# Turning the operands of the gate-up product in the middle steps of a float32 feed-forward layer

## The chip, the cores and the metric

The kernel runs on one core of one Trainium2 chip. The metric is the device time of the whole program in microseconds, the median of several runs. Only TensorE multiplies; VectorE (DVE), ScalarE (ACT) and GpSimd (POOL) do the rest; SyncE (SP) issues the weight transfers.

## The reference

Two transformer-like blocks run one after the other on 256 tokens of width 1024, all in float32. What the change touches is the feed-forward layer, which occurs four times (ffn1 and ffn2 in each of two layers):

```python
D_FF = 2816
def swiglu(x, w_in, w_out):          # x: 256 x 1024
    h = x @ w_in                     # w_in: 1024 x 5632
    gate, up = h[..., :D_FF], h[..., D_FF:]
    return (jax.nn.silu(gate) * up) @ w_out
x = layer_norm(ALPHA * x + 0.5 * swiglu(x, ffn_w_in[l], ffn_w_out[l]), g, b)
```

The rest (two kinds of attention, a state-space mixer with a pooling mixer, stick-breaking attention and two mixtures of experts) is not touched.

## The kernel before

Every float32 product of the dense layers is made of three TensorE matmuls (mm3, lines 657 to 661). Each operand is split into a high part, which ACT copies (fp32r), and a low part, which DVE gets as operand minus high part. high x high, high x low and low x high are added up in PSUM. The first operand of mm3 is the stationary one (loaded into the array by an LDWEIGHTS), the second one moves through it. The profile prints a matmul as out<-moving,stationary, so hh<-w_hi,xt_hi has the weights moving.

Weights come in units of 128 x 2048 floats (1 MB) through a ring of six buffers. SP loads them, waiting on unit_used. For each unit ACT makes w_hi (split, L1477), DVE makes w_lo (L1934), and PE uses it when lo_ready counts it.

A feed-forward layer is eleven steps over 256 columns of D_FF each. gated in the PE program runs a first step, then nine middle steps with step(j), j = 1 to 9 (three written out and three rounds of two in a loop; in the fourth layer all nine are written out, since parts of the later state-space mixer, s5_weights, run beside them), and a last step with an order of its own. A middle step of PE before the change is:

- tile(h_bank, half=first_half): two units of 4 x 128 rows of the input dimension; for both token tiles t of 128 tokens, x turned (xt) is stationary, 128 x 128, and 512 columns of weights (256 gate, 256 up) move. That is 2 units x 2 tiles x 4 row blocks x 3 = 48 matmuls of 512 columns. h_bank[t] holds tokens by features. first_half is raised when t = 0 is complete.
- down(j == 1, False): the product of step j-1 with w_out, 24 matmuls of 512 columns. It waits for ht_lo_ready.
- turn_h(): waits for h_ready and turns h(j) with four 128 x 128 transposes (L792) into turn_bank[0].

ACT does per step: split, silus (Silu of the gate half of each bank, L1495; the second waits for the end of the tile), split, high_h (waits for h_turned, copies the turned h out of PSUM as ht_hi, L1505), split. DVE does: split, product(t) twice (up times gate, L1966, raises h_ready), split, low_h (ht_lo = turned h minus ht_hi, L1953, raises ht_lo_ready), split. h is used by PE one step later, in down of the next step, so the step has a pipeline of its own.

In the fourth layer s5_weights puts four more transposes (L845) behind down and four ahead of the next tile for c = 0 to 3, i.e. around the turn_h of steps 6 to 9. ACT copies the first four out of turn_bank[1] (L1729, win_copied) before PE may issue the second four. After step 1 and step 2 of some layers ACT and DVE do side work of other layers (aside).

Of the kernel before, what the change touches and what calls it, by code (L numbers as in the profile page):

```python
# [26 lines left out]
P = 128  # L27
T = 256
# [101 lines left out]
def program(nc, a, out):  # L130
    with ExitStack() as ctx:
# [533 lines left out]
        def _(pe):  # L665
# [76 lines left out]
            def tile(banks, half=None, middle=None):  # L742

                for u in range(2):
# [6 lines left out]
                            mm.then_inc(half, 1)  # L751
                    mm.then_inc(unit_used, 1)

            def narrow_tile(banks):

                w = unit(KD)
                for t in range(TT):
                    for k in range(KD):
                        mm = mm3(pe, banks[t][:, 0:256], xt_part(k, t), (w[0][:, k], w[1][:, k]), k == 0, k == KD - 1)
                mm.then_inc(unit_used, 1)  # L760
# [88 lines left out]
            def gated(ready, beside=None):  # L849
                peeled = FF_PEELED if beside is None else FF_STEPS - 2  # L850

                def step(j):
                    if beside is not None:
                        beside(j, 0)
                    tile(h_bank, half=first_half)
                    if beside is not None:
                        beside(j, 1)
                    down(j == 1, False)
                    if beside is not None:
                        beside(j, 2)  # L860
                    turn_h()
                first_tile(h_bank, half=first_half, second=lambda: turn_x(1, ready=ready), by_halves=ready is None)
                turn_h()
                for j in range(1, peeled + 1):
                    step(j)
                if beside is None:
                    with seen.loop(FF_ROUNDS, [(lo_ready, 6), (h_ready, 2 * TT), (ht_lo_ready, 2)]):
                        step(FF_PEELED + 1)
                        step(FF_PEELED + 2)
                    n[0] += 6 * (FF_ROUNDS - 1)  # L870
                else:
                    beside(FF_STEPS - 1, 0)
                    pe.wait_ge(win_copied, 8)

                gate_up = []
                for u in range(2):
                    gate_up.append(unit(4))
                    mm = four(h_bank[0][:, :], gate_up[u], u, 0)
                mm.then_inc(first_half, 1)
                before = unit(2)  # L880
                pe.wait_ge(ht_lo_ready, seen(ht_lo_ready))
                for c in range(2):
                    half_down(before, 0, c, False, False)
                turn_half(0, turn_bank[0])
                half_down(before, 1, 0, False, False)
                final = unit(2)
                pe.wait_ge(ht_lo_ready, seen(ht_lo_ready))
                for c in range(2):
                    half_down(final, 0, c, False, True).then_inc(y_half, 1)
                for u in range(2):  # L890
                    four(h_bank[1][:, :], gate_up[u], u, 1).then_inc(unit_used, 1)
                half_down(before, 1, 1, False, False).then_inc(unit_used, 1)
                turn_half(1, h_bank[0])
                turn_x(0)
                pe.wait_ge(ht_lo_ready, seen(ht_lo_ready))
                half_down(final, 1, 0, False, True).then_inc(y_half, 1)
                half_down(final, 1, 1, False, True).then_inc(unit_used, 1)
# [565 lines left out]
        def _(act):  # L1463
# [29 lines left out]
            def gated(aside=(), beside=None):  # L1493
                def silu(t):
                    act.activation(gate_act[:, t], h_bank[t][:, 0:HALF], ACT.Silu).then_inc(gate_ready, 1)  # L1495

                def silus():
                    act.wait_ge(first_half, seen(first_half))
                    silu(0)
                    act.wait_ge(unit_used, seen.ahead(unit_used, 2))  # L1500
                    silu(1)

                def high_h():
                    act.wait_ge(h_turned, seen(h_turned))
                    act.activation(ht_hi[:, :, :].rearrange("p k t -> p (k t)"), turn_bank[0][:, :], ACT.Copy)\  # L1505
                        .then_inc(ht_hi_ready, 1)

                def high_half(t, bank_):
                    act.wait_ge(h_turned, seen(h_turned))
                    act.activation(ht_hi[:, :, t * P:(t + 1) * P], bank_[:, 0:2 * P].rearrange("p (k c) -> p k c", k=2),  # L1510
                                   ACT.Copy).then_inc(ht_hi_ready, 1)

                def step():
                    split()
                    silus()
                    split()
                    high_h()
                    split()
                    seen(unit_used, 3)

                high_xt(1)
                split_to(3)
                silus()
                split_to(4)
                high_h()
                seen(unit_used, 2)
                for j in range(1, (FF_PEELED if beside is None else FF_STEPS - 2) + 1):
                    ahead = peeled_splits(j)
                    split_to(ahead[0])
                    if beside is not None:  # L1530
                        beside(j, 0)
                    silus()
                    if beside is not None:
                        beside(j, 1)
                    split_to(ahead[1])
                    if beside is not None:
                        beside(j, 2)
                    high_h()
                    split_to(ahead[2])
                    seen(unit_used, 3)  # L1540
                    if j <= len(aside):
                        aside[j - 1]()
                if beside is None:
                    with seen.loop(FF_ROUNDS, [(s, 32) for s in unit_loaded] + [(unit_used, 6), (first_half, 2), (h_turned, 2)]):
                        step()
                        step()
                    n[0] += 6 * (FF_ROUNDS - 1)
                else:
                    beside(FF_STEPS - 1, 0)

                act.wait_ge(first_half, seen(first_half))
                silu(0)
                high_half(0, turn_bank[0])
                split_to(FF_UNITS + 2)
                wait_units(FF_UNITS - 2)
                silu(1)
                high_half(1, h_bank[0])
                high_xt(0)
                split_to(FF_UNITS + 3)
                stage_done(FF_UNITS)  # L1560

            def high_block(t, b, bank_):
                act.wait_ge(x_turned, seen(x_turned))
# [356 lines left out]
        def _(dve):  # L1920
# [30 lines left out]
            def low_h():  # L1951
                dve.wait_ge(ht_hi_ready, seen(ht_hi_ready))
                dve.tensor_tensor(ht_lo[:, :, :].rearrange("p k t -> p (k t)"), turn_bank[0][:, :],  # L1953
                                  ht_hi[:, :, :].bitcast(F32).rearrange("p k t -> p (k t)"), ALU.subtract)\
                    .then_inc(ht_lo_ready, 1)

            def low_half(t, bank_):
                dve.wait_ge(ht_hi_ready, seen(ht_hi_ready))
                at = (slice(None), slice(None), slice(t * P, (t + 1) * P))
                dve.tensor_tensor(ht_lo[at], bank_[:, 0:2 * P].rearrange("p (k c) -> p k c", k=2), ht_hi[at].bitcast(F32),  # L1960
                                  ALU.subtract).then_inc(ht_lo_ready, 1)

            def gated(k, aside=(), looped=True):
                def product(t):
                    dve.wait_ge(gate_ready, seen(gate_ready))
                    dve.tensor_tensor(h[:, t], h_bank[t][:, HALF:2 * HALF], gate_act[:, t], ALU.mult).then_inc(h_ready, 1)  # L1966

                def step():
                    split()
                    for t in range(TT):  # L1970
                        product(t)
                    split()
                    low_h()
                    split()

                low_xt(1)
                product(0)
# [4 lines left out]
                for j in range(1, (FF_PEELED if looped else FF_STEPS - 2) + 1):  # L1982
                    ahead = peeled_splits(j)
                    split_to(ahead[0])
                    for t in range(TT):
                        product(t)
                    split_to(ahead[1])
                    low_h()
                    split_to(ahead[2])
                    if j <= len(aside):  # L1990
                        aside[j - 1]()
                if looped:
                    with seen.loop(FF_ROUNDS, [(hi_ready, 6), (gate_ready, 2 * TT), (ht_hi_ready, 2)]):
                        step()
                        step()
                    n[0] += 6 * (FF_ROUNDS - 1)
# [870 lines left out]
```

## Time and profile before

| | |
|---|---|
| median of 3 runs | 1763.74 us (1763.15 to 1764.32) |
| the profiled execution | 1767.34 us |
| span from its first to its last instruction | 1765.5 us |
| mean granted TensorE clock | 0.988 of full |
| TensorE matmul busy | 1701.7 us, 96% |
| TensorE weight load busy | 1231.0 us, 70% |
| VectorE busy | 920.4 us, 52% |
| ScalarE busy | 631.0 us, 36% |

A matmul's duration in the trace (0.39 us for one of 512 columns) is longer than the distance to the next one, because they are pipelined; what a matmul costs is the distance from start to start.

### The profile page before, as it was taken

To read this page: it belongs to the slowest core of one execution; us is meant where nothing else is said; L and a number is where in the kernel's file an instruction comes from. 1 tells how busy PE (TensorE), PEld (TensorE's weight loads), DVE (VectorE), ACT (ScalarE), POOL (GpSimd) and SP (SyncE) were. 2 spreads that over 40 slices of the span, in tenths; PEclk is the share of its full clock that TensorE was granted. 3 is DMA by queue.
4 is the path that set the end of the run, shared out by engine and by line. 5 is a ranking of instruction groups with operands and counts; after the bars stand their busy time and mean duration, and the time that the engine had idled before them with its cause. 6 is when DMAs were issued, how large, how long until landed. Compare 5 with 4: busy or idle time off the path is not lost.

```text
span 1765.5 us, 21660 instructions
## 1 busy us (share of the span) xinstructions
PE 1701.7 (96%) x8720; PEld 1231.0 (70%) x8720; DVE 920.4 (52%) x1314; ACT 631.0 (36%) x825; POOL 107.8 (6%) x89
## 2 busy tenths in 40 slices
PE   7999999999999999999999998999998999999996
PEld 5888877778878888867887787744443777644442
DVE  4655656675555545776676587511113667511113
ACT  4544443354424443443454364211112344211110
POOL 1000060000000000332000000000000000000000
PEclk9999998999999999999999999999999999999999
DMA  7555550545555554514554352899999432999995
GB/s 293 177 189 189 196 181 6 197 184 190 190 183 197 187 181 170 211 63 171 191 184 172 122 211 102 347 418 420 427 428 410 173 143 108 357 418 427 428 426 241
DMA packets 47810, 419.77 MB, mean 238 GB/s; under 512 B 5392, under 2 KB 5392, under 8 KB 9456
## 3 DMA queue, kind: packets, MB, share of 16 engines
q1 hardware_dynamic: 44208, 405.82, 59.0%
q0 software_dynamic: 3520, 12.78, 2.1%
q8 instruction: 61, 1.00, 0.2%
q14 instruction: 21, 0.17, 0.0%
HBM read 417.53 MB, written 1.05 MB: 237 GB/s over the span
## 4 chain that ended last, share of the span: by engine, by line
PE 84%; DVE 7%; DMA 4%; ACT 3%; POOL 1%; issue 1%; SPq 0%; DVEq 0%; POOLq 0%; ACTq 0%
PE hh L1294 11%; PE y L659 10%; PE y L661 10%; PE y L660 10%; PE hh L659 8%; PE hh L661 8%; PE hh L660 8%; PE hh L1326 3%; PE turn L1204 3%; DMA wide<-pairs 3%; PE turn L1326 3%; DVE w_lo L1934 2%; PE y L1338 1%; ACT w_hi L1477 1%; PE turn L792 1%; PE y L954 1%
## 5 line engine op out<-in xcount | busy, mean ns | idle before, releaser
L1934 DVE TENSOR_TENSOR w_lo<-raw,w_hi 128x2048 fp32r<-128x2048 f32 x180 | 408.8, 2288 | 140.3 <-ACT w_hi L1477 139.6
L1477 ACT ACTIVATE w_hi<-raw 128x2048 fp32r<-128x2048 f32 x192 | 363.1, 1912 | 61.4 <-DMA raw<-units 61.3
L659 PE MATMUL hh<-w_hi,xt_hi 128*128 128x512 f32 x704 | 280.3, 398 | 8.6 <-DVE w_lo L2714 3.0
L661 PE MATMUL hh<-w_hi,xt_lo 128*128 128x512 f32 x704 | 275.9, 392 | 0.0
L660 PE MATMUL hh<-w_lo,xt_hi 128*128 128x512 f32 x704 | 275.6, 391 | 0.0
L1294 PE MATMUL hh<-wide,work 128*64 128x512 f32 x880 | 195.7, 594 | 3.1 <-DMA wide<-pairs 3.1
L659 PE MATMUL y<-w_hi,xt_hi 128*128 128x512 f32 (+1 forms) x464 | 184.0, 397 | 5.0 <-DVE xt_lo L2483 3.1
L660 PE MATMUL y<-w_lo,xt_hi 128*128 128x512 f32 (+1 forms) x464 | 179.8, 387 | 0.0
L661 PE MATMUL y<-w_hi,xt_lo 128*128 128x512 f32 (+1 forms) x464 | 179.6, 387 | 0.0
L659 PEld LDWEIGHTS hh<-w_hi,xt_hi 128*128 128x128 f32 x704 | 133.1, 189 | 37.5 <-issue 3.4
L661 PEld LDWEIGHTS hh<-w_hi,xt_lo 128*128 128x128 f32 x704 | 133.0, 189 | 28.6
L660 PEld LDWEIGHTS hh<-w_lo,xt_hi 128*128 128x128 f32 x704 | 133.2, 189 | 26.4
L1294 PEld LDWEIGHTS hh<-wide,work 128*64 128x64 f32 x880 | 61.5, 137 | 123.1 <-issue 116.8
L659 PE MATMUL y<-w_hi,ht_hi 128*128 128x512 f32 x368 | 145.0, 394 | 2.2 <-DVE w_lo L1934 2.0
L661 PE MATMUL y<-w_hi,ht_lo 128*128 128x512 f32 x368 | 143.4, 390 | 0.0
L660 PE MATMUL y<-w_lo,ht_hi 128*128 128x512 f32 x368 | 143.4, 390 | 0.0
L1495 ACT ACTIVATE gate_h<-hh 128x256 f32<-128x256 f32 x88 | 33.4, 383 | 213.7 <-PE hh L661 213.5
L659 PEld LDWEIGHTS y<-w_hi,xt_hi 128*128 128x128 f32 x464 | 88.7, 191 | 25.2 <-DVE xt_lo L2483 3.5
L599 POOL TENSOR_TENSOR rstd<-moments,minus_half 128x1 f32<-128x1 f32 x20 | 20.4, 1018 | 1330.5 <-DVE moments L2027 811.1
L661 PEld LDWEIGHTS y<-w_hi,xt_lo 128*128 128x128 f32 x464 | 88.6, 191 | 17.8
L660 PEld LDWEIGHTS y<-w_lo,xt_hi 128*128 128x128 f32 x464 | 88.9, 192 | 16.1
L2649 DVE TENSOR_TENSOR slot_mem<-hh,slot_mem 128x512 fp32r<-128x512 f32 x16 | 11.1, 691 | 142.2 <-ACT slot_mem L1861 142.2
(366 smaller groups left out, 1983.5 us busy)
## 6 DMA issues: line engine op xcount, KB each, us to landing
raw<-units SPq DMA_DIRECT2D x192, 1024.0 KB
wide<-pairs SPq DMA_DIRECT2D x81, 2048.0 KB
wide<-pairs SPq DMA_DIRECT2D x8, 1024.0 KB, 9.4
late<-pairs SPq DMA_DIRECT2D x7, 1024.0 KB
raw<-pairs SPq DMA_DIRECT2D x7, 1024.0 KB
spare<-pairs SPq DMA_DIRECT2D x2, 2048.0 KB
xt_wide<-pairs SPq DMA_DIRECT2D x2, 2048.0 KB
ln_gb<-ln_g POOLq DMA_DIRECT2D x6, 512.0 KB, 4.0
```

Of the source, the lines that this page charges most:

```text
L599: pool.tensor_tensor(rstd[:, t], moments[:, t, 1:2], minus_half[:, 0:1], ALU.pow).then_inc(rstd_ready, 1)
L659: pe.matmul(dst, left[0], right[0], start=start, stop=False)
L660: pe.matmul(dst, left[0], right[1], start=False, stop=False)
L661: return pe.matmul(dst, left[1], right[0], start=False, stop=stop)
L792: mm = pe.transpose(turn_bank[0][:, k * T + t * P:k * T + (t + 1) * P], h[:, t, k * P:(k + 1) * P], ident[:, :])
L954: mm = pe.matmul(dst, pt1[:, i % 2, c * T + kt_ * P:c * T + (kt_ + 1) * P], v1[:, kt_, cols], start=kt_ == 0, stop=kt_ == 1)
L1204: mm = pe.matmul(dst[:, k * P:(k + 1) * P], x[:, t, at * P:(at + 1) * P], pick[:, p, t, :], start=t == 0, stop=t == TT - 1)
L1294: mm = pe.matmul(dst[half(b), :], xe[:, p, 4 * u + k, half(b)], w[b][:, k, :], start=u == 0 and k == 0, stop=u == 1 and k == 3)
L1326: mm = pe.matmul(dst[half(b), :], turned[:, k, half(b)], w[b][:, k, :], start=k == 0, stop=k == 3)
L1477: act.activation(hi[r][:, :], raw[r][:, :], ACT.Copy).then_inc(hi_ready, 1)
L1495: act.activation(gate_act[:, t], h_bank[t][:, 0:HALF], ACT.Silu).then_inc(gate_ready, 1)
L1934: dve.tensor_tensor(lo[r][:, :], raw[r][:, :], hi[r][:, :].bitcast(F32), ALU.subtract)\
```

## The change

In step(j), tile is replaced by turned_tile, and turn_h by a wait for h_ready. In turned_tile the 128 x 128 blocks of weights are stationary and xt moves, all 256 tokens at once. The result is features by tokens, already in the layout that turn_h made: h_bank[0] holds the gate (m = 0, 1), h_bank[1] the up part (m = 2, 3). The tile is 2 units x 4 m x 4 k x 3 = 96 matmuls of 256 columns. ACT makes one Silu over 128 x 512 (silu_all) and copies ht_hi from h in SBUF (high_all), waiting for the end of down of the step before, since that reads ht_hi. DVE makes one product over 128 x 512 (product_all), which waits for the end of the tile, and ht_lo from h in SBUF (low_all). First and last steps keep their code, apart from waits in product(t). The core of the diff:

```diff
+            def turned_tile():
+                for u in range(2):
+                    w = unit(4)
+                    order = [(m, k) for k in range(4) for m in range(4)] if u == 0 else [(m, k) for m in range(4) for k in range(4)]
+                    for m, k in order:
+                        dst = h_bank[m // 2][:, (m % 2) * T:(m % 2 + 1) * T]
+                        mm = mm3(pe, dst, [v[:, k, m * P:(m + 1) * P] for v in w], (xt_hi[:, 4 * u + k, :], xt_lo[:, 4 * u + k, :]),
+                                 u == 0 and k == 0 and m % 2 == 0, u == 1 and k == 3 and m % 2 == 1)
+                        if u == 1 and m == 1 and k == 3:
+                            mm.then_inc(first_half, 1)
+                    mm.then_inc(unit_used, 1)
...
-                    tile(h_bank, half=first_half)
+                    turned_tile()
...
                     down(j == 1, False)
...
-                    turn_h()
+                    pe.wait_ge(h_ready, seen(h_ready))
...
+                def silu_all():
+                    act.wait_ge(first_half, seen(first_half))
+                    act.activation(gate_act.rearrange("p t c -> p (t c)"), h_bank[0], ACT.Silu).then_inc(gate_ready, 1)
+                def high_all():
+                    act.wait_ge(h_ready, seen(h_ready))
+                    act.wait_ge(unit_used, seen.ahead(unit_used, 3))
+                    act.activation(ht_hi[:, :, :].rearrange("p k t -> p (k t)"), h.rearrange("p t c -> p (t c)"), ACT.Copy)\
+                        .then_inc(ht_hi_ready, 1)
...
+                def product_all():
+                    dve.wait_ge(gate_ready, seen(gate_ready))
+                    dve.wait_ge(unit_used, seen.ahead(unit_used, 2))
+                    dve.wait_ge(ht_lo_ready, seen.ahead(ht_lo_ready, 0))
+                    dve.tensor_tensor(h.rearrange("p t c -> p (t c)"), h_bank[1], gate_act.rearrange("p t c -> p (t c)"),
+                                      ALU.mult).then_inc(h_ready, 1)
+                def low_all():
+                    dve.wait_ge(ht_hi_ready, seen(ht_hi_ready))
+                    dve.tensor_tensor(ht_lo[:, :, :].rearrange("p k t -> p (k t)"), h.rearrange("p t c -> p (t c)"),
+                                      ht_hi[:, :, :].bitcast(F32).rearrange("p k t -> p (k t)"), ALU.subtract)\
+                        .then_inc(ht_lo_ready, 1)
```

In the steps of ACT and DVE, silus, high_h, the two product(t) and low_h give way to these. The counts in the loops follow.

## Rows read from the trace of the kernel before

**Rows 1.** Page: busy time, share of the span, instructions of TensorE's matmuls.

```profile
PE 1701.7 (96%) x8720; PEld 1231.0 (70%) x8720; DVE 920.4 (52%) x1314; ACT 631.0 (36%) x825; POOL 107.8 (6%) x89
```

**Rows 2.** Page: the chain that ended last, by engine.

```profile
PE 84%; DVE 7%; DMA 4%; ACT 3%; POOL 1%; issue 1%; SPq 0%; DVEq 0%; POOLq 0%; ACTq 0%
```

**Rows 3.** Groups by line: the four transposes of turn_h; busy, mean ns | idle before.

```profile
L792 PE MATMUL turn<-ident_r,gate_h 128*128 128x128 f32 x168 | 25.3, 273 | 3.7 <-DVE gate_h L1966 3.7
```

**Rows 4.** Timeline of PE, first layer: start us, us, engine, line, out<-in.

```profile
99.66 0.39 PE L659 MATMUL hh<-w_hi,xt_hi 128*128 128x512 f32 x1
...
113.72 0.39 PE L661 MATMUL y<-w_hi,ht_lo 128*128 128x512 f32 x1
113.95 0.60 PE L792 MATMUL turn<-ident_r,gate_h 128*128 128x128 f32 x4
114.30 0.48 PE L659 MATMUL hh<-w_hi,xt_hi 128*128 128x512 f32 x1
...
130.75 0.60 PE L792 MATMUL turn<-ident_r,gate_h 128*128 128x128 f32 x4
```

**Rows 5.** Timeline of PE: turn_h of steps 2 and 9 of the first layer.

```profile
63.53 0.60 PE L792 MATMUL turn<-ident_r,gate_h 128*128 128x128 f32 x4
...
181.16 0.60 PE L792 MATMUL turn<-ident_r,gate_h 128*128 128x128 f32 x4
```

**Rows 6.** Timeline of PE: stationary weights, moving xt (state-space mixer), then 512 columns.

```profile
1047.25 0.28 PE L660 MATMUL y<-xt_lo,w_hi 128*128 128x256 f32 x1
...
1049.87 0.28 PE L661 MATMUL y<-xt_hi,w_lo 128*128 128x256 f32 x1
...
1076.14 0.28 PE L660 MATMUL hh<-xt_lo,w_hi 128*128 128x256 f32 x1
...
1081.64 0.28 PE L661 MATMUL hh<-xt_hi,w_lo 128*128 128x256 f32 x1
1081.77 0.40 PE L659 MATMUL y<-w_hi,xt_hi 128*128 128x512 f32 x1
...
1084.29 0.39 PE L661 MATMUL y<-w_hi,xt_lo 128*128 128x512 f32 x1
```

**Rows 7.** Timeline of PE: stationary xt, 256 columns of weights moving (narrow_tile).

```profile
241.69 0.28 PE L660 MATMUL y<-w_lo,xt_hi 128*128 128x256 f32 x1
...
246.37 0.28 PE L660 MATMUL y<-w_lo,xt_hi 128*128 128x256 f32 x1
```

**Rows 8.** Windows: us, busy of PE, PEld, DVE, ACT, POOL, clock, DMA, GB/s.

```profile
1076.14:1081.66 5.52, 5.52 (x48) 5.52 (x48) 4.40 (x7) 3.47 (x5) 0.00 (x0) 1.00 0.34 140
114.30:125.30 11.00, 11.00 (x51) 9.11 (x50) 5.61 (x4) 4.71 (x4) 0.00 (x0) 1.00 0.50 191
```

**Rows 9.** Timeline of PE, ACT, DVE: step 2 of the first and second layers.

```profile
45.74 0.60 PE L792 MATMUL turn<-ident_r,gate_h 128*128 128x128 f32 x4
46.38 0.60 ACT L1505 ACTIVATE ht_hi<-turn 128x512 fp32r<-128x512 f32 x1 [3.69 <-PE turn L792]
47.01 0.69 DVE L1953 TENSOR_TENSOR ht_lo<-turn,ht_hi 128x512 fp32r<-128x512 f32 x1 [1.99 <-ACT ht_hi L1505]
...
57.95 0.50 PE L659 MATMUL y<-w_hi,ht_hi 128*128 128x512 f32 x1 [0.71 <-DVE w_lo L1934]
...
368.71 0.50 PE L659 MATMUL y<-w_hi,ht_hi 128*128 128x512 f32 x1 [1.31 <-DVE w_lo L1934]
```

**Rows 10.** Timeline of PE and ACT, fourth layer: around the turn_h of step 6.

```profile
936.95 0.60 PE L792 MATMUL turn<-ident_r,gate_h 128*128 128x128 f32 x4
937.15 0.60 ACT L1729 ACTIVATE work<-turn 128x512 f32<-128x512 f32 x1 [3.03 <-PE turn L845]
...
937.80 0.66 PE L845 MATMUL turn<-ident_r,work 128*128 128x128 f32 x4 [0.25 <-ACT work L1729]
```

**Rows 11.** Timeline of ACT and DVE: the second Silu and product of that step.

```profile
108.71 0.38 ACT L1495 ACTIVATE gate_h<-hh 128x256 f32<-128x256 f32 x1 [2.34 <-PE hh L661]
...
109.12 0.43 DVE L1966 TENSOR_TENSOR gate_h<-hh,gate_h 128x256 f32<-128x256 f32 x1 [2.29 <-ACT gate_h L1495]
```

More of the change, by code:

```diff
@@ L866, in gated @@
                 if beside is None:
-                    with seen.loop(FF_ROUNDS, [(lo_ready, 6), (h_ready, 2 * TT), (ht_lo_ready, 2)]):
+                    with seen.loop(FF_ROUNDS, [(lo_ready, 6), (h_ready, 2), (ht_lo_ready, 2)]):
                         step(FF_PEELED + 1)
@@ L1514, in step @@
                     split()
-                    silus()
+                    silu_all()
                     split()
-                    high_h()
+                    high_all()
                     split()
@@ L1526, in gated @@
                 seen(unit_used, 2)
+                seen(h_ready, TT)
                 for j in range(1, (FF_PEELED if beside is None else FF_STEPS - 2) + 1):
@@ L1531, in gated @@
                         beside(j, 0)
-                    silus()
+                    silu_all()
                     if beside is not None:
@@ L1537, in gated @@
                         beside(j, 2)
-                    high_h()
+                    high_all()
                     split_to(ahead[2])
@@ L1543, in gated @@
                 if beside is None:
-                    with seen.loop(FF_ROUNDS, [(s, 32) for s in unit_loaded] + [(unit_used, 6), (first_half, 2), (h_turned, 2)]):
+                    with seen.loop(FF_ROUNDS, [(s, 32) for s in unit_loaded] + [(unit_used, 6), (first_half, 2), (h_ready, 2)]):
                         step()
@@ L1560, in gated @@
                 stage_done(FF_UNITS)
+                seen(h_ready, TT)
             def high_block(t, b, bank_):
@@ L1955, in low_h @@
                     .then_inc(ht_lo_ready, 1)
+                seen(ht_lo_ready)
             def low_half(t, bank_):
@@ L1961, in low_half @@
                                   ALU.subtract).then_inc(ht_lo_ready, 1)
+                seen(ht_lo_ready)
             def gated(k, aside=(), looped=True):
@@ L1965, in product @@
                     dve.wait_ge(gate_ready, seen(gate_ready))
+                    if seen.ahead(ht_lo_ready, 0):
+                        dve.wait_ge(ht_lo_ready, seen.ahead(ht_lo_ready, 0))
                     dve.tensor_tensor(h[:, t], h_bank[t][:, HALF:2 * HALF], gate_act[:, t], ALU.mult).then_inc(h_ready, 1)
+                def product_all():
+                    dve.wait_ge(gate_ready, seen(gate_ready))
+                    dve.wait_ge(unit_used, seen.ahead(unit_used, 2))
+                    dve.wait_ge(ht_lo_ready, seen.ahead(ht_lo_ready, 0))
+                    dve.tensor_tensor(h.rearrange("p t c -> p (t c)"), h_bank[1], gate_act.rearrange("p t c -> p (t c)"),
[5 more added lines that the diff above has]
+                        .then_inc(ht_lo_ready, 1)
+                    seen(ht_lo_ready)
                 def step():
                     split()
-                    for t in range(TT):
-                        product(t)
+                    product_all()
                     split()
-                    low_h()
+                    low_all()
                     split()
+                    seen(unit_used, 3)
+                seen(unit_used, base[0] + 2 - seen.n.get(id(unit_used), 0))
                 low_xt(1)
@@ L1984, in gated @@
                     split_to(ahead[0])
-                    for t in range(TT):
-                        product(t)
+                    product_all()
                     split_to(ahead[1])
-                    low_h()
+                    low_all()
                     split_to(ahead[2])
+                    seen(unit_used, 3)
                     if j <= len(aside):
@@ L1992, in gated @@
                 if looped:
-                    with seen.loop(FF_ROUNDS, [(hi_ready, 6), (gate_ready, 2 * TT), (ht_hi_ready, 2)]):
+                    with seen.loop(FF_ROUNDS, [(hi_ready, 6), (gate_ready, 2), (ht_hi_ready, 2), (ht_lo_ready, 2), (unit_used, 6)]):
                         step()
```

## The prediction

> **What bounds the kernel now.** I read the page's busy times first, then the chain that ended last, the groups by line, and PE's timeline through one middle step. TensorE is busy 96% of the span, and 84% of the chain is PE [rows 1, 2]. The busy share could still hide idle time behind modelled ends, so the timeline decides. In a middle step the 62 distances from 99.66 to 113.72 make 14.06 us, 0.2268 us a matmul of 512 columns, with no gap between tile and down [rows 4]. Seven steps take 181.16 - 63.53 = 117.63 us, 16.804 us each [rows 5]. 48 + 24 = 72 matmuls are 16.327 us of that. The other 0.477 us is the turn: 113.95 to 114.30 for the four transposes, 0.35 us, and 0.13 us in the slower first matmuls behind them. PE waited for the product only four times ahead of these transposes, 3.7 us in all, and those are the turns of the four first steps, which stay [rows 3]. So the middle steps are bound by what PE issues, and the sum is made of PE start-to-start distances.
>
> **The tile.** 36 middle steps (nine in each of four layers) trade 48 matmuls of 512 columns for 96 of 256. The columns that move are the same; the weight loads double. The trace of before has this very form, stationary weights with xt moving, in the state-space mixer: 46 distances from 1076.14 to 1081.64 make 5.50 us, 0.1196 us each, and this run alternates its destination between the halves of both hh banks, as the new first unit does [rows 6]. A shorter run, 22 distances from 1047.25 to 1049.87, gives 0.1191 [rows 6]; the other orientation at 256 columns gives 4.68/39 = 0.1200 [rows 7]. I take 0.1196, the longest run of the same form, with 0.1191 and 0.1200 as ends. A tile becomes 96 x 0.1196 = 11.48 us against 48 x 0.2268 = 10.89 us, +0.594 us (+0.55 to +0.63). Times 36: +21.4 us (+19.8 to +22.9).
>
> In the run of 256 columns the weight loads fill the window, 5.52 of 5.52 us, where in the 512-column tile they take 9.11 of 11.00 [rows 8]. So the load of the next weights has no slack left there. The cost behind it can be read: the first 512-column matmuls after that run come 1081.64 to 1084.29, 2.65 us for one distance of 0.12 and eleven of 0.2268 (2.61), so 0.04 us is lost where the lead is rebuilt [rows 6]. This happens between tile and down in 32 steps (in four of the fourth layer other transposes already stand there): +1.3 us (0 to +1.6).
>
> The Trainium skill ("TensorE: Matmul & The Clock Gate", Back-to-back issue gap) gives N/2.4 + 2.5 ns warm, 109.2 ns at 256 columns and 215.8 at 512. An estimate by that page would put the tile at only 96 x 0.1092 - 48 x 0.2158 = +0.12 us; the trace disagrees at both sizes (0.1196 and 0.2268), and the sum goes by the trace. The same page says that in a stream of pairs both the load and the matmul set the spacing, which agrees with the filled load row in [rows 8].
>
> **The turns.** Of 40 such turns in the feed-forward layers 36 go, and in 32 of them the whole 0.477 us goes from PE's path: -15.3 us. Bounds: -11.2 us if only the 0.35 us goes and slow first matmuls stay, -15.3 otherwise. I take the far end, since down follows tile without loss when nothing lies between [rows 4]. In the fourth layer the turns of steps 6 to 9 lie between two sets of s5 transposes. ACT's copy starts at 937.15 and releases PE at 937.80 whatever PE does meanwhile; PE was already idle 0.25 us there [rows 10]. Removing the turn lengthens that idle time: 0 us saved, four times.
>
> **Two stalls shorten.** In step 2 of the first and second layers PE waits for w_lo 0.71 and 1.31 us [rows 9]. That wait ends a chain: turn at 45.74, ACT's ht_hi at 46.38, DVE's ht_lo at 47.01, then splits and side work on DVE. Now ACT needs no turn. It starts when down has ended, about 0.2 us after 45.74 (the last down matmul starts 0.23 before and lasts 0.39), instead of 0.64 after it, so the chain comes about 0.45 us earlier, and that step shortens by 0.45 instead of growing by 0.12: -0.57 us twice, -1.1 us (0 to -1.6).
>
> **ACT and DVE.** Two Silus of 0.38 us become one of 512 columns, between 0.38 and 0.60 (ACT's 512-column copy [rows 9]); two products of 0.43 become one, 0.43 to 0.86, nearest the 0.69 us of DVE's other 512-column operation with PSUM [rows 9, 11]. I take 0.60 and 0.69. ht_hi and ht_lo from SBUF: 0.60 and 0.69 at most. product_all waits for the tile's end; before, the second product did the same through the second Silu, starting at 109.12 and ending at 109.55, 4.4 us ahead of the turn at 113.95 [rows 4, 11]. The new one needs no Silu behind the tile and ends at about 109.4. Behind it on DVE stands the next split, as before. high_all waits for down's end; behind it on ACT stands a split, which comes some 0.4 us earlier than now. All of this lies beside down (24 x 0.2268 = 5.44 us) and the next tile: 0 us. If that cover went, each step would pay the part of about 1.1 us that sticks out. SP's loads still follow unit_used at the half and the end of a tile.
>
> **Sum.** +21.4 +1.3 -15.3 -1.1 = +6.3 us: 1767.34 of the profiled execution becomes 1773.6. That execution is 3.6 us above the median of 1763.74, which becomes 1770.0 us, 0.36% slower. About 0.2%, 3.5 us, is what a measurement of this kernel can tell from no change.
>
> **Rivals.**
> - Two matmuls of 256 columns cost one of 512, since the array is bound by columns. Then the tile and its transition cost nothing and the turns and stalls alone count: -16.4, 1747.3 us, faster. For it: equal columns, and TensorE's clock stands at 1.00 in both windows, its 2.4 GHz level [rows 8]. Against it: three runs at 0.119 to 0.120. It decides below 0.1181 us a matmul, where 96 of them cost 48 of 512 plus the 0.45 us that turns, stalls and transitions give back per step; the lowest run seen is 0.1191. Chance 0.06. The page's gap above is a milder form: its +0.12 a tile would give 4.3 - 15.3 - 1.1 = -12.1 us, an estimate by that page, 1751.6.
> - The tile runs at 0.1191 and down loses nothing: 19.8 - 16.4 = +3.4, 1767.1 us, no difference that can be told. Chance 0.12.
> - The turn's time comes back as something else, a wait for h_ready or slow first matmuls at the same place: 0.13 to 0.48 us in 32 steps, +4 to +15 us on the forecast, 1774 to 1785. For it: a new wait stands where the turn was. Against it: 4.4 us of slack. Chance 0.06.
>
> **How the numbers follow.** The forecast has 0.76, its own range 1767.8 to 1772.5, from the ends of the pitch (-1.6, +1.5) and those of transition and stalls. For 8 in 10 the range takes in the second rival and the mild end of the third: 1766.3 to 1773.5. Slower by over 0.2%: 0.82; within: 0.12; faster: 0.06.
>
> **What would show it.** PE's timeline should have 256-column hh matmuls 0.1196 apart, down at 0.2268 with 0.04 lost at its start, no L792 transposes but in first steps, and a step of 11.48 + 5.44 + 0.04 = 16.96 us against 16.80. In the fourth layer steps 6 to 9 PE's idle time ahead of the second s5 transposes should grow from 0.25 to about 0.7 us. The waits on w_lo in step 2 should be near 0.15 and 0.75. A pitch under 0.118 or over 0.121, a wait on h_ready in steps 1 to 9, or any new w_lo wait would make the prediction wrong.

## The result and the profile after

The changed kernel takes 1771.12 us (median of 6 runs, 1769.73 to 1772.76) where the kernel before takes 1763.45 us (median of 6, 1761.02 to 1764.95): ratio 1.0037, 95% interval 1.0023 to 1.0052, so 4 to 9 us slower. The profiled execution took 1771.89 us, span 1770.2.

The page's busy line answers to [rows 1]: PE is as busy as before, in 1584 more matmuls, and the weight loads went from 1231.0 to 1303.9 us.

```profile
PE 1703.1 (96%) x10304; PEld 1303.9 (74%) x10304; DVE 917.5 (52%) x1278; ACT 628.5 (36%) x789; POOL 107.8 (6%) x89
```

PE's timeline through a middle step answers to [rows 4]: start us, us, engine, line, out<-in.

```profile
97.66 0.28 PE L659 MATMUL hh<-xt_hi,w_hi 128*128 128x256 f32 x1
97.77 0.28 PE L660 MATMUL hh<-xt_lo,w_hi 128*128 128x256 f32 x1
97.89 0.28 PE L661 MATMUL hh<-xt_hi,w_lo 128*128 128x256 f32 x1
...
109.05 0.28 PE L661 MATMUL hh<-xt_hi,w_lo 128*128 128x256 f32 x1
109.17 0.40 PE L659 MATMUL y<-w_hi,ht_hi 128*128 128x512 f32 x1
...
114.41 0.39 PE L661 MATMUL y<-w_hi,ht_lo 128*128 128x512 f32 x1
114.64 0.28 PE L659 MATMUL hh<-xt_hi,w_hi 128*128 128x256 f32 x1
...
131.62 0.28 PE L659 MATMUL hh<-xt_hi,w_hi 128*128 128x256 f32 x1
```

95 distances from 97.66 to 109.05 are 0.1199 us each, the tile is 11.51 us, down 5.47 us, and the step (114.64 to 131.62) 16.98 us against 16.804 before [rows 5]. No transposes stand between down and the next tile, and nothing waits there. In the window of one tile (columns as in [rows 8]) the weight loads are busy without a break:

```profile
114.64:126.15 11.51, 11.51 (x97) 11.51 (x96) 5.28 (x3) 5.23 (x5) 0.00 (x0) 1.00 0.52 182
```

The waits on w_lo in step 2 of the first and second layers, answering to [rows 9], and PE and ACT around the place of the turn of step 6 in the fourth layer, answering to [rows 10]:

```profile
58.13 0.50 PE L659 MATMUL y<-w_hi,ht_hi 128*128 128x512 f32 x1 [0.19 <-DVE w_lo L1960]
...
365.49 0.50 PE L659 MATMUL y<-w_hi,ht_hi 128*128 128x512 f32 x1 [0.81 <-DVE w_lo L1960]
...
936.88 0.60 PE L858 MATMUL turn<-ident_r,work 128*128 128x128 f32 x4
937.52 0.60 ACT L1755 ACTIVATE work<-turn 128x512 f32<-128x512 f32 x1 [3.02 <-PE turn L858]
938.26 0.30 PE L858 MATMUL turn<-ident_r,work 128*128 128x128 f32 x1 [0.78 <-ACT work L1755]
```

**Two executions compared.** The nine middle steps of the four layers, from the start of the first middle tile to the start of the last step's tile in each timeline:

| kernel | layer 1 | layer 2 | layer 3 | layer 4 | sum |
|---|---|---|---|---|---|
| before | 152.21 | 152.84 | 151.23 | 162.35 | 618.6 |
| changed | 153.35 | 153.98 | 152.90 | 165.60 | 625.8 |

That is +7.2 us, while the spans differ by 4.7 us only. The table leaves out one small gain: in the first three layers the last step no longer starts behind transposes, and its first tile part is 0.11 to 0.14 us shorter (5.44 us against 5.55 to 5.58), 0.4 us in all. Most of what is left of the difference lies in two stretches whose code is the same but for that. Their windows in before and then in the changed kernel say (us, PE busy, clock, DMA, GB/s):

```profile
181.50:325.57 144.07, 139.94 (x732) 0.95 0.36 129
...
997.50:1765.50 768.00, 732.50 (x4076) 0.99 0.77 316
```

```profile
182.56:322.09 139.53, 135.31 (x730) 0.99 0.38 133
...
999.75:1770.20 770.45, 733.18 (x4076) 0.98 0.77 315
```

In the profiled execution of before, TensorE's clock was granted at 0.95 over the first attention and it took 144.07 us; in that of the changed kernel at 0.99, and it took 139.53. Since the code there is the same and the clock differs, this part is not the change. In the last stretch it is the other way round, by 2.45 us, and 1.36 us of that stand in one place, the first tile part of the fourth layer's last step (24 matmuls of 512 columns; before, then changed, same columns as above):

```profile
997.50:1003.12 5.62, 5.62 (x25) 1.00 0.06 23
```

```profile
999.75:1006.73 6.98, 6.98 (x25) 0.78 0.05 19
```

In the changed kernel the clock falls to its lower level (1.2 GHz) there, and six distances in a row are 0.42 to 0.59 us instead of 0.22 to 0.35. PE was idle before it for 0.78 and 2.08 us, in the kernel before for 0.25 and 2.11 us. Whether the longer idle time of the changed kernel brings this on is not shown: e0, the same kernel again, has the fall at the same place (6.98 us at 0.78), e4 and e7 have it too, and e3, whose late steps are as before the change, has none, but e1, e2, e5 and e6 below, where the turn stands in these steps, have it as well.

Differences of this kind lie in the runs too (23 runs of the kernel before on one chip went from 1761.5 to 1771.9), so in the experiments the steps of the trace are read first and the ratio second.

### The profile page after: what moved, and what is told of

It reads as the page before. It is cut to its first block, busy times and chain, and to the rows that moved or that the text cites. A ratio compares the mean times of both kernels' runs of the same rounds, so it can differ in the third digit from the quotient of the medians.

```text
span 1770.2 us, 24842 instructions
## 1 busy us (share of the span) xinstructions
PE 1703.1 (96%) x10304; PEld 1303.9 (74%) x10304; DVE 917.5 (52%) x1278; ACT 628.5 (36%) x789; POOL 107.8 (6%) x89
## 4 chain that ended last, share of the span: by engine, by line
PE 84%; DVE 7%; DMA 4%; ACT 3%; issue 1%; POOL 1%; SPq 0%; DVEq 0%; POOLq 0%; ACTq 0%
PE hh L1307 11%; PE y L659 10%; PE y L660 10%; PE y L661 10%; PE hh L659 9%; PE hh L661 9%; PE hh L660 9%; DMA wide<-pairs 3%; PE hh L1339 3%; PE turn L1217 3%; PE turn L1339 3%; DVE w_lo L1960 2%; PE y L1351 1%; ACT w_hi L1490 1%; DMA raw<-units 1%
## 5 line engine op out<-in xcount | busy, mean ns | idle before, releaser
L659 PE MATMUL hh<-xt_hi,w_hi 128*128 128x256 f32 x1168 | 331.0, 283 | 0.0
L660 PE MATMUL hh<-xt_lo,w_hi 128*128 128x256 f32 x1168 | 330.5, 283 | 0.0
L661 PE MATMUL hh<-xt_hi,w_lo 128*128 128x256 f32 x1168 | 330.5, 283 | 0.0
L659 PEld LDWEIGHTS hh<-xt_hi,w_hi 128*128 128x128 f32 x1168 | 224.1, 192 | 1.2
L660 PEld LDWEIGHTS hh<-xt_lo,w_hi 128*128 128x128 f32 x1168 | 224.1, 192 | 1.1
L661 PEld LDWEIGHTS hh<-xt_hi,w_lo 128*128 128x128 f32 x1168 | 224.1, 192 | 0.0
L659 PEld LDWEIGHTS y<-w_hi,ht_hi 128*128 128x128 f32 x368 | 69.2, 188 | 16.7 <-DVE w_lo L1960 1.4
```

The source lines that it names most:

```text
L659: pe.matmul(dst, left[0], right[0], start=start, stop=False)
L660: pe.matmul(dst, left[0], right[1], start=False, stop=False)
L661: return pe.matmul(dst, left[1], right[0], start=False, stop=stop)
```

## The experiments

The diffs are shortened to their core, and in those of e2 and e4 to e7 words stand in for longer expressions of the code.

**e1: the turn put back.**

```diff
                     pe.wait_ge(h_ready, seen(h_ready))
+                    for k in range(2):
+                        for t in range(TT):
+                            pe.transpose(turn_bank[0][:, k * T + t * P:k * T + (t + 1) * P], h[:, t, k * P:(k + 1) * P], ident[:, :])
```

> The changed kernel, with four 128x128 transposes of h put back where turn_h stood in the nine middle steps (their result is read by nobody). Theory (the turn costs 0.48 us on PE's path: 0.35 for the transposes and 0.13 in the first matmuls behind them; in steps 6 to 9 of the fourth layer nothing): 32 x 0.48 = +15.3 us on the changed kernel's 1771.1, so 1786.4, ratio to the kernel before 1.013. Step in the trace 17.46 us instead of 16.98. Rival (256-column matmuls don't feel the transposes ahead of them): 32 x 0.35 = +11.2, 1782.3, step 17.33. Rival (the turn was hidden): 1771.

Measured: 1784.27 us, ratio 1.0108 (1.0085 to 1.0130). The timeline of PE:

```profile
98.52 0.60 PE L877 MATMUL turn<-ident_r,gate_h 128*128 128x128 f32 x4
98.87 0.36 PE L659 MATMUL hh<-xt_hi,w_hi 128*128 128x256 f32 x1
99.07 0.28 PE L660 MATMUL hh<-xt_lo,w_hi 128*128 128x256 f32 x1
...
115.93 0.38 PE L877 MATMUL turn<-ident_r,gate_h 128*128 128x128 f32 x2
```

The step is 17.41 us. The four transposes cost 0.35 us of PE's path, and the tile behind them 11.59 instead of 11.51, so 0.43 us: between the two forecasts, since a 256-column tile loses less behind transposes (0.08) than a 512-column one (0.13). The middle steps sum to 638.5 us, 12.6 more than the changed kernel. In the fourth layer two late steps stand 19.53 us apart (transposes at 950.54 and 970.07) against 19.60 without the turn: nothing is paid for it there. So the turn is hidden in these four steps, as the prediction had it. In step 2 of the first and second layers e1 pays next to nothing either (17.43 and 18.10 us against 17.43 and 18.06), since nobody waits for its transposes and they only fill time in which PE waits for w_lo. Where ACT's ht_hi waits for the turn, as in before and in e2, the same steps take 17.79 and 18.41 us (before) and 17.78 and 18.41 (e2).

**e2: the old operands, twice as many matmuls.**

```diff
-                    tile(h_bank, half=first_half)
+                    halved_tile(h_bank, half=first_half)     # per k, for c in range(2):
+    mm3(pe, banks[t][:, c*T:(c+1)*T], xt_part(4*u+k, t), [v[:, k, c*T:(c+1)*T] for v in w], ...)
```

> The kernel before, its operands as they were (xt stationary, weights moving), its turns in place, but each 512-column matmul of the middle tiles cut into two of 256 columns. Theory (what costs is twice as many matmuls with a 128-column load each, whichever operand is stationary): 96 x 0.1200 - 48 x 0.2268 = +0.63 us a tile, 36 x 0.63 + 36 x 0.04 behind the tile = +24 us, 1787.6, ratio 1.014; distance in the trace 0.1200. Rival (the cost comes from the exchange of operands itself, weights read by the load and xt by the moving side): no change, 1763.5.

Measured: 1784.20 us, ratio 1.0109 (1.0085 to 1.0133). PE's timeline and the window of one tile:

```profile
98.66 0.60 PE L806 MATMUL turn<-ident_r,gate_h 128*128 128x128 f32 x4
99.02 0.36 PE L659 MATMUL hh<-w_hi,xt_hi 128*128 128x256 f32 x1
...
116.08 0.38 PE L806 MATMUL turn<-ident_r,gate_h 128*128 128x128 f32 x2
```

```profile
99.02:110.61 11.59, 11.59 (x100) 11.59 (x99) 5.70 (x4) 4.69 (x4) 0.00 (x0) 1.00 0.53 183
```

The tile is 11.59 us and the step 17.42, the same as e1's to 0.01 us, though the operands stand the other way round. Which operand is stationary costs nothing; the count of matmuls and loads is what costs, and e2 doesn't tell these two apart. The forecast was 36 steps of 0.67, +24 us. Measured are 17.42 - 16.80 = 0.61 us a step, since the 256-column tile loses 0.08 us behind the transposes where a 512-column one loses 0.13, and 639.1 us for the middle steps, +20.5.

**e3: the fourth layer's steps 6 to 9 as before.** PE, ACT and DVE choose by step:

```diff
+                    turned = beside is None or j <= 5
-                    turned_tile()
+                    if turned: turned_tile()
+                    else: tile(h_bank, half=first_half)      # and turn_h, silus, product(t), high_h, low_h
```

> The changed kernel, but steps 6 to 9 of the fourth layer as in the kernel before (tile, turn_h, two Silus, two products). Theory (there the turn is hidden behind ACT's copy of s5 work, so the exchange is all cost, +0.62 us a step): -2.5 us on the changed kernel's 1771.1, so 1768.6, ratio to before 1.0029; those steps 18.98 us again instead of 19.60. Rival (the turn costs there too): within 0.5 us of 1771.1.

Measured: 1767.93 us, ratio 1.0017 (1.0002 to 1.0032). The turns of steps 6 and 7 stand at 934.41 and 953.39, 18.98 us apart again, and the middle steps sum to 623.6 us, 2.2 below the changed kernel. The theory holds in the steps; the medians' difference of 3.2 us is within what they scatter.

**e4 and e7: what the load costs.** In e4 each matmul of the turned tile moves 128 columns instead of 256, with its load of 128, and there are twice as many; in e7 it moves 256 with a load of 64.

```diff
# e4
+  for t in range(TT): mm3(pe, dst[:, t*P:(t+1)*P], [v[:, k, m*P:(m+1)*P] for v in w], xt_part(4*u+k, t), ...)
# e7
-  mm3(pe, dst,           [v[:, k, m*P:(m+1)*P] for v in w], ...)
+  mm3(pe, dst[0:P // 2], [v[:, k, m*P:m*P + P//2] for v in w], ...)
```

> The changed kernel with each 256-column matmul of the turned tile cut into two of 128 columns, 192 a tile, each with its load of 128 columns. Theory (the load of the weights sets the distance once the columns are few): 0.111 us a matmul, as the 128-column gathers with a 128-column load show in the trace before, tile 21.3 us, +9.8 us a tile, 2124 us. Rival (a fixed cost of 13 ns a matmul over its columns, 0.067 us): tile 12.8 us, 1819 us.

> The changed kernel with 64 instead of 128 weight columns stationary in every matmul of the turned tiles; it leaves out half of the features of the middle steps. The moving side keeps its 256 columns. Theory (a part of the 0.120 is the load, which has no lead left): the distance falls to at most 0.116, which the router's matmuls with 16 stationary columns show, tile 11.1 us, 36 x -0.4 = -14 us, 1757. Rival (the cost over the columns is fixed per matmul): 0.120, 1771.

Measured, one run each: e4 2125.31 us, e7 1750.19 us. The window of one tile of e4, then of e7:

```profile
108.99:130.38 21.39, 21.39 (x193) 21.38 (x192) 9.59 (x5) 10.23 (x7) 0.00 (x0) 1.00 0.29 99
```

```profile
112.15:123.04 10.89, 10.89 (x97) 10.88 (x96) 5.28 (x3) 5.25 (x5) 0.00 (x0) 1.00 0.53 193
```

A matmul of e4 takes 21.39 / 192 = 0.1114 us. By its 128 moving columns alone it would take about half of e7's price, 0.057 us (an estimate), so this is taken as the load's own rate for 128 columns. One of e7 takes 10.89 / 96 = 0.1134 us, half of the 0.2268 of 512 columns to the last digit, and its tile is as long as 48 matmuls of 512 columns (48 x 0.2268 = 10.89). So 256 columns do cost half of 512, as long as the load isn't in the way; with a load of 128 columns they cost 0.1200. The theory of e7 had the direction and too small a size: its nine middle steps in four layers sum to 604.9 us, 21.0 less than e0's, where the theory had 14 less. The changed kernel's whole loss in the tile, 11.51 - 10.89 = 0.62 us, goes with the load of 128 columns. Two things stay open. e7 halves the columns loaded and the rows of the result together, so it can't tell a cheaper load from a cheaper half-wide result. And 0.1200 lies above both 0.1114 and 0.1134: neither the load nor the columns alone set it, and why the two don't overlap fully no run shows. Both busy columns are full in e7 too, at the pace of the moving columns, so a full PEld alone does not tell which of the two sets the pace; a run with a smaller load does.

**e5 and e6: fewer loads in the turned form.** xt_hi and xt_lo are laid out side by side, so that w_hi, loaded once, meets both in 512 columns; DVE adds the two halves of each bank.

```diff
+  pe.matmul(banks[m] as 2 x T, w_hi[:, k, m*P:(m+1)*P], xt_both[:, :, 4*u+k, :], start=u == 0 and k == 0, stop=False)
+  mm = pe.matmul(banks[m][:, 0:T], w_lo[:, k, m*P:(m+1)*P], xt_hi[:, 4*u+k, :], start=False, stop=u == 1 and k == 3)
...
+  dve.tensor_reduce(gate_act, h_pair[0][:, :, :].rearrange("p b (a t) -> p b t a", a=2), AX_X, ALU.add)
```

> A new form of the turned tile: xt_hi and xt_lo lie side by side, and w_hi, loaded once, meets both in one matmul of 512 columns; w_lo meets xt_hi in one of 256. The two halves of each bank are summed by DVE afterwards (two tensor_reduce of 1024 elements, about 1.1 us each by elements against 0.69 for 512), before Silu and before the product; it uses the banks of turn too. Steps 6 to 9 of the fourth layer as in the kernel before. Theory (a 512-column matmul 0.2268, a 256-column one 0.1200): tile 32 x 0.3468 = 11.10 us, +0.21 on the kernel before, 32 times +6.8; turns -15.3; stalls -0.7; sum about -9, 1754.5, ratio 0.995. Rival 1 (behind a 512-column matmul the load has lead, and 256 columns cost 0.116): tile 10.97, 1750. Rival 2 (DVE's two sums, +2 us a step, make the product or w_lo late): waits on h_ready or w_lo in the steps, 1765 or more.

Measured: 1771.79 us, ratio 1.0039 (1.0022 to 1.0055). PE's timeline:

```profile
96.95 0.40 PE L766 MATMUL hh<-xt_both,w_hi 128*128 128x512 f32 x1
97.19 0.28 PE L767 MATMUL hh<-xt_both,w_lo 128*128 128x256 f32 x1
97.31 0.40 PE L766 MATMUL hh<-xt_both,w_hi 128*128 128x512 f32 x1
97.55 0.28 PE L767 MATMUL hh<-xt_both,w_lo 128*128 128x256 f32 x1
```

None of the three theories had it. 32 pairs take 11.29 us, 0.3528 a pair instead of 0.3468: in turns, the 512-column matmul is followed after 0.236 us on average and the 256-column one after 0.117. The reading that the 256-column neighbour leaves the next load no lead (no time in which it can run ahead of its own matmul) is put to the test in e6. The step is 16.79 us, no better than before. Step 1 of each layer grew by 1.1 us, where the tile has to wait for ht_lo of the first step before it may write turn_bank[0] (3.3 us of such waits in all). DVE's sums take 1.22 us each. They make DVE's product late in one step of the fourth layer, beside the side work, and the next tile waits for it:

```profile
900.48 0.50 PE L766 MATMUL hh<-xt_both,w_hi 128*128 128x512 f32 x1 [0.83 <-DVE gate_h L2052]
```

From the start of down to this tile 6.50 us pass instead of 5.50, so the theory of a late DVE is true in that one place. In step 3 of the first layer, beside side work too, 5.72 us pass instead of 5.50; the profile of e5 names no releaser for it, but that of e6 names the product there. In no other middle step does PE lose time between down and tile. Over all middle steps the sum is 623.4 us, 4.7 more than before. e6 groups the matmuls by eight and mends step 1:

```diff
+  for half in range(2):
+      for m in (2*half, 2*half+1): for k in range(4): (the 512-column matmul)
+      for m in (2*half, 2*half+1): for k in range(4): (the 256-column matmul)
...
+                        if j == 1: turned_tile()
+                        else: paired_tile()
```

> The paired form again (w_hi against xt_hi and xt_lo in one matmul of 512 columns), with two repairs: the 512-column matmuls and the 256-column ones stand in runs of eight instead of taking turns, and step 1 uses the turned tile, so that no tile waits for ht_lo of the first step; in the fourth layer steps 2 to 4 are paired, step 1 turned, 5 to 9 as before the change. Theory (taking turns costs because no load gets a lead: 0.3528 us a pair against 0.2268 + 0.1200): tile 11.1 to 11.2 us instead of 11.29, step 16.6 to 16.7 against 16.80 before, sum over 27 paired steps -3 to -5, four turned steps +1, stalls -0.7: 1759 to 1761 where the kernel before has 1763.5, ratio 0.997 to 0.999. Rival (every matmul with a 256-column neighbour costs the same, whatever the order): tile 11.29, ratio 1.000 to 1.001.

Measured: 1758.40 us, ratio 0.9965 (0.9951 to 0.9979), faster than both kernels. One tile of its timeline:

```profile
114.13 1.98 PE L763 MATMUL hh<-xt_both,w_hi 128*128 128x512 f32 x8
115.95 1.11 PE L767 MATMUL hh<-xt_both,w_lo 128*128 128x256 f32 x8
116.90 2.00 PE L763 MATMUL turn<-xt_both,w_hi 128*128 128x512 f32 x8
118.74 1.12 PE L767 MATMUL turn<-xt_both,w_lo 128*128 128x256 f32 x8
...
125.28 0.40 PE L660 MATMUL y<-w_hi,ht_hi 128*128 128x512 f32 x1
```

The tile is 11.14 us, and starts of down stand 16.61 us apart (108.67 to 125.28), 0.19 less than before. So the order alone took 0.15 us off the tile, as the theory had it. The middle steps sum to 615.9 us, 2.7 below before; the fourth layer alone is 0.9 us longer than before, since DVE's sums again make the product late in its step 4:

```profile
892.77 0.50 PE L660 MATMUL hh<-w_hi,xt_both 128*128 128x512 f32 x1 [1.00 <-DVE gate_h L2056]
```

The medians differ by 5.5 us. A part of what the steps don't account for goes with the clock: all 12 runs of e6 had a mean granted clock of 0.991 or more, of the 23 runs of before on this chip only 13 had, and the median of these 13 is 1762.3 us, 3.9 above e6. In e5 the same choice leaves 5.2 us of the 7.4 between the medians, near the 4.7 of its steps. The last 1.2 us of e6 stay without a name.

**e0: the changed kernel on the chip of e6.**

> The changed kernel itself, unedited, on the same chip as the next ones. If chips differ by no more than their runs do, its ratio to the kernel before stays in 1.0023 to 1.0052; by the steps of the traces (middle steps together +7.1 us) it should be 1.0040.

Measured: 1770.67 us, ratio 1.0034 (1.0021 to 1.0047); its middle steps sum to 625.9 us. The result holds, and the steps repeat to 0.1 us.

## Why the prediction was right

- **The tile.** Forecast 11.48 us, measured 11.51. The run I took 0.1196 from starts with short distances, eight in 0.94 us, and the other 38 are 0.1200 each:

```profile
1077.09 0.28 PE L659 MATMUL hh<-xt_hi,w_hi 128*128 128x256 f32 x1
```

In the new tile only the first two are short (0.113 and 0.119), and all later ones are 0.1200. That loads issued ahead make these first distances short is argued, not shown. The sum was 0.03 x 36 = 1.1 us too small here. The cause, doubled loads, was argued from the filled load row; that row was full in e7 too and proves nothing by itself. e2 shows that the exchange of operands is not the cause, and e7 that the cost goes with the load of 128 columns.
- **Tile to down.** Forecast 0.04 us, measured 5.47 - 5.44 = 0.03.
- **The turns.** Forecast 0.48 us in 32 steps and nothing in four. A regular step is 16.98 us against a forecast of 16.96; PE's idle time ahead of the second s5 transposes grew from 0.25 to 0.78 us (forecast about 0.7), and steps 7 and 8 grew by 0.62 us (19.60 against 18.98), steps 6 and 9 by about 0.5 and 0.6. e1 and e3 agree.
- **The two stalls.** Forecast -0.45 us for those steps, measured 17.43 against 17.79 and 18.06 against 18.41, -0.36 and -0.35. ht_hi starts 0.26 us behind the place where the turn stood (46.53 against 46.27), not 0.2, and its copy from SBUF takes 0.63 us where I had put 0.60 as the most. This term was 0.2 us in all too large. Its working also had a slip: by its own terms such a step would have grown by 0.16 us, not 0.12.
- **ACT and DVE.** 0.60 us for Silu and 0.69 for the product, as taken, and no wait on h_ready in the middle steps.
- **The sum.** +6.3 us forecast. Its terms answer to +7.2 in the middle steps less the 0.4 at the starts of the last steps, so about +6.8. The medians are 7.7 apart; the 1.36 us of the lower clock in the fourth layer's last step were in no term. That 7.7 lies so near to the sum of the steps has some luck in it, with a scatter of several us between runs. By the rival of free 256-column matmuls it would have been -16: e7 shows its price for the tile right, 0.1134 us, and its condition missing, a load that fits under 256 columns.
- **The milder form of that rival.** The Trainium skill ("TensorE: Matmul & The Clock Gate", Back-to-back issue gap) gives N/2.4 + 2.5 ns as the gap of an isolated matmul. By the prediction's estimate that would have made -12.1 us, a faster kernel too. The traces' 0.1200 us at 256 columns and 0.2268 at 512 decide against it here.

## What to carry to other kernels

Price a matmul by its distance in a long run of the same form, and leave out the run's first distances, which can be shorter. Exchanging the operands to save a transpose has a price if each matmul then moves half the columns: here 48 loads more a tile cost 0.62 us, and the turn gave back 0.48. Matmuls with fewer moving columns cost least when they stand together (e6 against e5), and the better exchange is the one in which a loaded block meets more columns, as in e6.

## What the runs showed that I had not expected

- Distances in these traces in fp32r at a granted clock of 1.00: 0.2268 us for 512 moving columns, 0.1200 for 256 with a load of 128 columns, 0.1134 for 256 with a load of 64, 0.1114 for 128 with a load of 128.
- Order alone changes the price: 32 matmuls of 512 and 32 of 256 columns cost 11.29 us a tile in turns and 11.14 in runs of eight.
- A tensor_reduce that adds pairs in PSUM, 1024 elements to 512, takes 1.22 us where an operation on 512 takes 0.69.
- A copy of 512 columns by ACT takes 0.63 us from SBUF and 0.60 from PSUM.
